# Conditioning products in unsplit fp32, in four 32-column tiles of the array

## The chip, the cores and the metric

The kernel runs on one NeuronCore of a Trainium2 chip. The metric is the device time of one execution in microseconds (us). All inputs and outputs are float32 in the chip's memory.

## What is computed

Two layers of a transformer-like block over 256 context rows and 256 latent rows of width 1024. Each layer runs a gated feed-forward, a mixer and a second feed-forward. All three are modulated and gated by vectors that come from a conditioning product, and this product is what the change is about:

```python
mx = (jax.nn.silu(c) @ w_mod[i] + b_mod[i]).reshape(bsz, N_MOD, d)...   # c: 1 x 1024, w_mod[i]: 1024 x 9216
mc = (jax.nn.silu(c_ctx) @ w_mod[i] + b_mod[i]).reshape(N_MOD, 1, 1, d) # c_ctx: 1024
u  = rmsnorm(h, g_pre) * (1 + scale) + shift                             # rows of mx or mc
y  = (silu(u @ wg) * (u @ wu)) @ wd                                      # wg, wu: 1024 x 2816, wd: 2816 x 1024
h  = h + 0.5 * gate * rmsnorm(y, g_post)
```

There are two conditioning vectors (context and latent), and the weights `w_mod` are 2 x 1024 x 9216 float32 values, 75 MB, of which each is used for two rows only.

## The kernel before

Activations lie with features on the 128 partitions and the 512 rows along the free dimension. Weights come from memory as **panels** of 1024 x 256 values (1 MB, 8 blocks of 128 rows of the inner dimension). A panel is used as two **halves** of 128 columns.

Products are made precise in split form: a value is the sum of a high part in the fast format fp32r and the remainder, also in fp32r. ScalarE copies a half panel to its high part (`weight_hi`, line 85), VectorE subtracts that from the raw panel (`weight_lo`, line 93; GpSimd does it in the mixer), and TensorE multiplies high by high, high by low and low by high (`product_half`, lines 132 to 134), 24 matmuls for a half with 8 blocks.

The conditioning products go the same way, panel by panel, between the halves of the feed-forwards, so that their transfers and splits run beside the weight products. There are 72 panels: 8 in the opening (`opening`), 22 in the up and gate loop of the first feed-forward of layer 0 and 6 in its down products, 22 and 10 in the second feed-forward of layer 0 (for layer 1), and 4 in the down products of the first feed-forward of layer 1. For each half panel:

- SP's queue asks for a panel into the one buffer `raw_mod` (`load_mod`) once both halves of the panel before are split.
- ScalarE makes the high part (`mod_hi`, line 174), once TensorE has finished with the one split buffer `mod_split`; VectorE makes the low part (`mod_lo`, line 180).
- TensorE multiplies (`mod_mm`, line 197): 8 matmuls, one for each block of the inner dimension. The weights are a 128 x 128 slice of `cond`, zero but for four columns: high and low part of the two conditioning vectors. The slice is shifted by four columns for each panel, so that panel n lands on rows 4n to 4n + 3 of the PSUM bank. The moving operand is high and low part of the half panel beside each other, 256 columns.

At the end of a group of panels VectorE adds the sums of high and low parts of the weights into `mod_rows` (`mod_rows_dve`, lines 207 and 209), TensorE turns them with two transposes (`mod_turn_pe`, line 216), and VectorE adds the bias and the two parts of the vectors (`mod_out_dve`, lines 227 and 231).

In the opening there are six stage buffers and the two weight buffers for the eight panels, and four split buffers. TensorE's order there is written out: the first panel, the transposes of x, two panels, then four rounds of column sums of squares and half a panel, parameters, a panel, the norm factors, two panels, the turn. TensorE's warm-up matmuls between stages are at line 415. Two other lines serve the prediction as measures: line 1233 (four products of fp32 operands with 128 x 128 weights for a mean over features, 512 columns in layer 0 and 256 in layer 1) and line 1209 (products in fp32r with 128 x 32 weights), both in the mixer.

## Time and profile before

| what | value |
|---|---|
| median of three runs | 2363.13 us |
| lowest and highest | 2362.87 and 2373.77 us |
| profiled execution, its own time | 2368.33 us |
| profiled execution, span | 2366.6 us |
| mean granted clock of TensorE | 0.964 of full speed |
| TensorE, VectorE, ScalarE, GpSimd busy | 2200.4, 1264.0, 986.5, 230.2 us |
| read from memory | 288.02 MB |

The span is the time from the first to the last instruction of the profiled execution. Busy time is the union of an engine's instructions. A matmul's listed duration includes the time that its results take to leave the array, which the next one overlaps; the time that it holds TensorE is read from one start to the next.

### The profile page before, as it was taken

To read this page: it belongs to the slowest core of one execution; us is meant where nothing else is said; L and a number is where in the kernel's file an instruction comes from. 1 tells how busy PE (TensorE), PEld (TensorE's weight loads), DVE (VectorE), ACT (ScalarE), POOL (GpSimd) and SP (SyncE) were. 2 spreads that over 40 slices of the span, in tenths; PEclk is the share of its full clock that TensorE was granted. 3 is DMA by queue.
4 is the path that set the end of the run, shared out by engine and by line. 5 is a ranking of instruction groups with operands and counts; after the bars stand their busy time and mean duration, and the time that the engine had idled before them with its cause. 6 is when DMAs were issued, how large, how long until landed. Compare 5 with 4: busy or idle time off the path is not lost. (4 is left out here: it accounts for less than half of the span.)

```text
span 2366.6 us, 29334 instructions
## 1 busy us (share of the span) xinstructions
PE 2200.4 (93%) x11949; PEld 1883.8 (80%) x11949; DVE 1264.0 (53%) x1859; ACT 986.5 (42%) x1521; POOL 230.2 (10%) x159
## 2 busy tenths in 40 slices
PE   5999999988988989899999999999998987889998
PEld 5788888876676768688888887888888766778998
DVE  5544444357769743644444445333335578855554
ACT  5444333244465343444443334222324444454443
POOL 0000000033322300100000000000001332300000
PEclk9999999989999989899999998999998999989999
DMA  6445554312242212255554432232422233334553
GB/s 233 146 163 160 161 172 157 98 56 72 91 125 85 76 54 89 89 169 165 165 160 161 159 107 71 89 107 89 157 93 74 72 108 98 108 116 126 187 182 129
DMA packets 282836, 291.09 MB, mean 123 GB/s; under 512 B 8318, under 2 KB 275534, under 8 KB 282702
## 3 DMA queue, kind: packets, MB, share of 16 engines
q1 hardware_dynamic: 281671, 286.95, 37.9%
q10 hardware_dynamic: 1031, 2.28, 0.3%
q8 instruction: 94, 1.54, 0.3%
q14 instruction: 40, 0.33, 0.0%
HBM read 288.02 MB, written 1.18 MB: 122 GB/s over the span
## 5 line engine op out<-in xcount | busy, mean ns | idle before, releaser
L85 ACT ACTIVATE split<-raw 128x1024 fp32r<-128x1024 f32 (+1 forms) x368 | 382.8, 1040 | 929.6 <-PE bank L134 917.4
L93 DVE TENSOR_TENSOR split<-raw,split 128x1024 fp32r<-128x1024 f32 (+1 forms) x304 | 364.2, 1198 | 704.0 <-ACT split L85 703.9
L132 PE MATMUL bank<-uh,split 128*128 128x512 f32 (+1 forms) x1344 | 488.3, 363 | 1.1 <-DVE split L93 1.1
L134 PE MATMUL bank<-uh,split 128*128 128x512 f32 (+1 forms) x1344 | 488.0, 363 | 0.0
L133 PE MATMUL bank<-ul,split 128*128 128x512 f32 (+1 forms) x1344 | 488.0, 363 | 0.0
L134 PEld LDWEIGHTS bank<-uh,split 128*128 128x128 f32 x1344 | 253.7, 189 | 40.1
L132 PEld LDWEIGHTS bank<-uh,split 128*128 128x128 f32 x1344 | 253.8, 189 | 38.2 <-issue 1.5
L133 PEld LDWEIGHTS bank<-ul,split 128*128 128x128 f32 x1344 | 253.8, 189 | 36.8
L132 PE MATMUL bank<-hh,split 128*128 128x256 f32 (+1 forms) x836 | 281.1, 336 | 1.5 <-DVE split L93 1.5
L133 PE MATMUL bank<-hl,split 128*128 128x256 f32 (+1 forms) x836 | 279.5, 334 | 0.0
L134 PE MATMUL bank<-hh,split 128*128 128x256 f32 (+1 forms) x836 | 279.4, 334 | 0.0
L132 PE MATMUL bank<-mix_uh,split 128*128 128x512 f32 (+1 forms) x608 | 233.1, 383 | 26.4 <-POOL split L100 15.9
L134 PE MATMUL bank<-mix_uh,split 128*128 128x512 f32 (+1 forms) x608 | 218.4, 359 | 0.0
L133 PE MATMUL bank<-mix_ul,split 128*128 128x512 f32 (+1 forms) x608 | 218.3, 359 | 0.0
L180 DVE TENSOR_TENSOR mod_split<-raw_mod,mod_split 128x1024 fp32r<-128x1024 f32 x128 | 156.5, 1223 | 63.4 <-ACT mod_split L174 63.3
L197 PEld LDWEIGHTS bank<-mod_split,cond 128*128 128x128 f32 x1152 | 158.4, 194 | 37.8 <-DVE mod_split L180 15.6
L197 PE MATMUL bank<-mod_split,cond 128*128 128x256 f32 x1152 | 164.7, 288 | 24.3 <-DVE mod_split L1965 12.3
L100 POOL TENSOR_TENSOR split<-raw,split 128x1024 fp32r<-128x1024 f32 x64 | 153.9, 2405 | 327.3 <-ACT split L85 327.3
L397 POOL TENSOR_TENSOR res<-res,y 128x256 f32<-128x256 f32 x35 | 26.2, 766 | 1527.8 <-DVE y L382 1527.6
L132 PEld LDWEIGHTS bank<-hh,split 128*128 128x128 f32 x836 | 159.1, 190 | 16.5 <-DVE split L93 1.0
L134 PEld LDWEIGHTS bank<-hh,split 128*128 128x128 f32 x836 | 159.1, 190 | 15.8
L174 ACT ACTIVATE mod_split<-raw_mod 128x1024 fp32r<-128x1024 f32 x128 | 135.1, 1056 | 87.6 <-DMA raw_mod<-in_w_mod 71.8
(231 smaller groups left out, 2969.4 us busy)
## 6 DMA issues: line engine op xcount, KB each, us to landing
raw_mod<-in_w_mod SPq DMA_DIRECT2D x64, 1024.0 KB, 4.8
raw<-in_ffn_w_gate SPq DMA_DIRECT2D x44, 1024.0 KB, 5.2
raw<-in_ffn_w_up SPq DMA_DIRECT2D x44, 1024.0 KB, 5.1
raw<-in_w_in SPq DMA_DIRECT2D x40, 1024.0 KB, 5.1
raw<-in_ffn_w_down SPq DMA_DIRECT2D x32, 1024.0 KB, 5.1
raw<-in_w_out SPq DMA_DIRECT2D x16, 1024.0 KB, 5.0
raw<-in_ffn_w_down SPq DMA_DIRECT2D x16, 768.0 KB, 4.3
decay<-cum_rows SPq DMA_DIRECT2D x48, 256.0 KB, 3.3
```

Of the source, the lines that this page charges most:

```text
L85: ins = K.nc.scalar.activation(K.wh[:, half, 0:kn, :], K.raw[:, slot, 0:kn, half * P:half * P + P], ACT.Copy)
L93: ins = K.nc.vector.tensor_tensor(K.wl[:, half, 0:kn, :], K.raw[:, slot, 0:kn, half * P:half * P + P], r32(K.wh[:, half, 0:kn, :]), ALU.su ...
L100: ins = K.nc.gpsimd.tensor_tensor(K.wl[:, half, 0:kn, :], K.raw[:, slot, 0:kn, half * P:half * P + P], r32(K.wh[:, half, 0:kn, :]), ALU.su ...
L132: K.nc.tensor.matmul(bank[:, 0:tn], K.wh[:, half, k, :], h, start=first and k == 0, stop=False)
L133: K.nc.tensor.matmul(bank[:, 0:tn], K.wh[:, half, k, :], l, start=False, stop=False)
L134: ins = K.nc.tensor.matmul(bank[:, 0:tn], K.wl[:, half, k, :], h, start=False, stop=last and k == kn - 1)
L174: ins = K.nc.scalar.activation(K.mod_split[:, 0], K.raw_mod[:, :, parity * P:parity * P + P], ACT.Copy)
L180: ins = K.nc.vector.tensor_tensor(K.mod_split[:, 1], K.raw_mod[:, :, parity * P:parity * P + P], r32(K.mod_split[:, 0]), ALU.subtract)
L197: ins = K.nc.tensor.matmul(out, cond, split[:, :, k, :], start=h == group_h and k == 0, stop=True, skip_group_check=True)
L397: ins = K.nc.gpsimd.tensor_tensor(K.res[:, j, t0:t0 + CTX], K.res[:, j, t0:t0 + CTX], y[:, j, a:a + CTX], ALU.add)
```

## The change

The conditioning products are no longer split. Their operands are plain fp32, and each of the 8 blocks of the inner dimension goes to one of four column tiles of the array: block k to output rows 32 (k mod 4) to 32 (k mod 4) + 31. The weights are a 128 x 32 slice of `cond`, zero but for the two conditioning vectors; the moving operand is a whole panel, 256 columns. So a panel takes 8 matmuls (in two rounds over the four tiles) instead of 16. A group with more than 16 panels uses both halves of the PSUM bank. The four tiles' partial sums are added in the turn: instead of transposes it multiplies the rows with a 128 x 32 matrix `fold` of four stacked identities. `mod_hi`, `mod_lo`, their buffers and signals go; there are two buffers `raw_mod`, and a panel is asked for when the panel before the last has been multiplied. The opening has eight stage buffers, the panels' order on TensorE is changed a little, and VectorE does the second ahead-of-time weight split after the bias. The rest of the kernel stays.

```diff
@@ -164,71 +164,60 @@
 
 def load_mod(K, sp, w_mod, q, panel):
 
-    sp.wait_ge(K.mod_lo.sem, K.mod_lo.at(2 * panel))
-    sp.dma_start(K.raw_mod[:, :, :], panel_src(w_mod, 0, 8, P * q)).then_inc(K.mod_full.inc(16), 16)
-
-
-def mod_hi(K, act, h, parity, panel):
-    act.wait_ge(K.mod_full.sem, K.mod_full.landed(panel + 1))
-    act.wait_ge(K.mod_mm.sem, K.mod_mm.at(h))
-    ins = K.nc.scalar.activation(K.mod_split[:, 0], K.raw_mod[:, :, parity * P:parity * P + P], ACT.Copy)
-    ins.then_inc(K.mod_hi_done.inc(), 1)
-
-
-def mod_lo(K, dve, h, parity):
-    dve.wait_ge(K.mod_hi_done.sem, K.mod_hi_done.at(h + 1))
-    ins = K.nc.vector.tensor_tensor(K.mod_split[:, 1], K.raw_mod[:, :, parity * P:parity * P + P],
-                                    r32(K.mod_split[:, 0]), ALU.subtract)
-    ins.then_inc(K.mod_lo.inc(), 1)
-
-
-COND_AT = P - 4
-
-
-def mod_mm(K, pe, h, split, group, group_h):
-
-    pe.wait_ge(K.mod_lo.sem, K.mod_lo.at(h + 1))
-    if h == group_h and group:
+    sp.wait_ge(K.mod_mm.sem, K.mod_mm.at(panel - 1))
+    sp.dma_start(K.raw_mod[:, panel % 2], panel_src(w_mod, 0, 8, P * q)).then_inc(K.mod_full[panel % 2].inc(16), 16)
+
+
+COL = 32
+GROUP_ROWS = COL // 2
+
+
+def mod_mm(K, pe, raw, panel, group, first):
+
+
+
+
+
+    if panel == first and group:
         pe.wait_ge(K.mod_row.sem, K.mod_row.at(group))
-    row, parity = 4 * ((h - group_h) // 2), h % 2
+    n = panel - first
+    row, region = 2 * (n % GROUP_ROWS), n // GROUP_ROWS
     for k in range(8):
-        cond = K.cond[:, COND_AT + P * k - row:COND_AT + P * k - row + P]
-        out = K.bank[4][:, parity * 2 * P:(parity + 1) * 2 * P].rearrange("p (w n) -> p w n", w=2)
-        ins = K.nc.tensor.matmul(out, cond, split[:, :, k, :], start=h == group_h and k == 0, stop=True, skip_group_check=True)
+        tile = COL * (k % 4)
+        cond = K.cond[:, COL - 2 + COL * k - row:2 * COL - 2 + COL * k - row]
+        out = K.bank[4][tile:tile + COL, region * 2 * P:(region + 1) * 2 * P]
+        ins = K.nc.tensor.matmul(out, cond, raw[:, k, :], start=n == 0 and k < 4, stop=True, skip_group_check=True)
     ins.then_inc(K.mod_mm.inc(), 1)
 
 
-def mod_rows_dve(K, dve, h, group):
-
-    dve.wait_ge(K.mod_mm.sem, K.mod_mm.at(h + 1))
+def mod_rows_dve(K, dve, panel, panels, group):
+
+    dve.wait_ge(K.mod_mm.sem, K.mod_mm.at(panel + 1))
     dve.wait_ge(K.mod_fold.sem, K.mod_fold.at(group))
-    parts = K.bank[4][:, :].rearrange("p (t w n) -> p w t n", w=2, n=P)
-    rows = K.rows[:, :].rearrange("p (t n) -> p t n", n=P)
-    K.nc.vector.tensor_copy(rows, parts[:, 0]).then_inc(K.mod_row_hi.inc(), 1)
-    dve.wait_ge(K.mod_row_hi.sem, K.mod_row_hi.at(group + 1))
-    K.nc.vector.tensor_tensor(rows, rows, parts[:, 1], ALU.add).then_inc(K.mod_row.inc(), 1)
-
-
-def mod_turn_pe(K, pe, group, bank=7):
+    cols = 2 * P * -(-panels // GROUP_ROWS)
+    K.nc.vector.tensor_copy(K.rows[:, 0:cols], K.bank[4][:, 0:cols]).then_inc(K.mod_row.inc(), 1)
+
+
+def mod_turn_pe(K, pe, panels, group, bank=7):
+
     pe.wait_ge(K.mod_row.sem, K.mod_row.at(group + 1))
-    pe.wait_ge(K.mod_evac.sem, K.mod_evac.at(2 * group))
-    for t in range(2):
-        ins = K.nc.tensor.transpose(K.bank[bank][:, t * P:t * P + P], K.rows[:, t * P:t * P + P], K.ident[:, :])
+    pe.wait_ge(K.mod_evac.sem, K.mod_evac.at(group))
+    for t in range(2 * -(-panels // GROUP_ROWS)):
+        ins = K.nc.tensor.matmul(K.bank[bank][:, t * COL:t * COL + COL], K.rows[:, t * P:t * P + P], K.fold[:, :], start=True, stop=True)
     ins.then_inc(K.mod_fold.inc(), 1)
 
 
 def mod_out_dve(K, dve, layer, q, panels, group, bank=7):
 
     dve.wait_ge(K.mod_fold.sem, K.mod_fold.at(group + 1))
-    turned = K.bank[bank][:, 0:2 * P].rearrange("p (t j i) -> p t j i", t=2, i=4)[:, :, 0:panels, :]
-    out = K.mod[:, layer, q:q + 2 * panels, :].rearrange("p (j t) s -> p t j s", t=2)
-    bias = K.par[:, layer, 0, q:q + 2 * panels].rearrange("p (j t) -> p t j", t=2)
-    for t in range(2):
-        ins = K.nc.vector.tensor_tensor(out[:, t], turned[:, t, :, 0:2], bias[:, t].unsqueeze(2).to_broadcast([P, panels, 2]), ALU.add)
-    ins.then_inc(K.mod_evac.inc(), 1)
-    dve.wait_ge(K.mod_evac.sem, K.mod_evac.at(2 * group + 1))
-    for t in range(2):
-        ins = K.nc.vector.tensor_tensor(out[:, t], out[:, t], turned[:, t, :, 2:4], ALU.add)
+    for region in range(-(-panels // GROUP_ROWS)):
+        n = min(panels - region * GROUP_ROWS, GROUP_ROWS)
+        turned = K.bank[bank][:, region * 2 * COL:(region + 1) * 2 * COL].rearrange("p (t j s) -> p t j s", t=2, s=2)[:, :, 0:n, :]
+        f = q + 2 * region * GROUP_ROWS
+        out = K.mod[:, layer, f:f + 2 * n, :].rearrange("p (j t) s -> p t j s", t=2)
+        bias = K.par[:, layer, 0, f:f + 2 * n].rearrange("p (j t) -> p t j", t=2)
+        for t in range(2):
+            ins = K.nc.vector.tensor_tensor(out[:, t], turned[:, t], bias[:, t].unsqueeze(2).to_broadcast([P, n, 2]), ALU.add)
     ins.then_inc(K.mod_evac.inc(), 1)
 
 
...
@@ -492,12 +481,14 @@
                     for i in range(len(self.streams)):
                         part(half, i, self.halves + n, self.first[p], False)
                 h = self.mod_h + n
-                if n < self.mods:
-                    mod_mm(K, pe, h, K.mod_split, self.mod_group, self.mod_h)
+                if half and n < self.mods:
+                    full = K.mod_full[h // 2 % 2]
+                    pe.wait_ge(full.sem, full.landed(h // 4 + 1))
+                    mod_mm(K, pe, K.raw_mod[:, h // 2 % 2], h // 2, self.mod_group, self.mod_h // 2)
                 if n == 0 and self.mod_group:
-                    mod_turn_pe(K, pe, 0)
+                    mod_turn_pe(K, pe, self.mod_h // 2, 0)
                 if self.mods and n == self.mods + 1:
-                    mod_turn_pe(K, pe, self.mod_group)
+                    mod_turn_pe(K, pe, self.mods // 2, self.mod_group)
                 n += 1
         nth = self.halves + n - 2
         for half in range(2):
...
         for n in range(2 * self.n_panels + 2):
-            p, half, h = n // 2, n % 2, self.mod_h + n
+            p, half = n // 2, n % 2
             if skip <= n < 2 * self.n_panels:
                 weight_hi(K, act, self.panels + p // 2, p % 2, half, self.parts[self.order[p][1]], self.halves + n)
             if n == 2:
                 act.wait_ge(K.pgain_ready.sem, K.pgain_ready.at(1))
-
-            if 1 <= n <= self.mods:
-                mod_hi(K, act, h - 1, 1 - half, (h - 1) // 2)
             if n >= 2 and self.last[p - 1] and self.order[p - 1][0] < 3:
                 j = 2 * self.order[p - 1][0] + half
                 act.wait_ge(K.half_done.sem, K.half_done.at(self.halves + n - 1))
...
         if mods_loop or mods_down:
-            K.raw_mod = mem.enter_context(nc.sbuf_tensor("raw_mod" + tag, [P, 8, 2 * P], F32))
-
-            K.mod_split = mem.enter_context(nc.sbuf_tensor("mod_split" + tag, [P, 2, 8, P], F32R))
-            K.rows = mem.enter_context(nc.sbuf_tensor("mod_rows" + tag, [P, 2 * P], F32))
+            K.raw_mod = mem.enter_context(nc.sbuf_tensor("raw_mod" + tag, [P, 2, 8, 2 * P], F32))
+            K.rows = mem.enter_context(nc.sbuf_tensor("mod_rows" + tag, [P, 4 * P], F32))
         hh = mem.enter_context(nc.sbuf_tensor("hh" + tag, [P, FT, tn], F32R))
         with ExitStack() as under:
             hf = under.enter_context(nc.sbuf_tensor("hf" + tag, [P, FT, tn], F32))
@@ -757,8 +741,10 @@
                     elif not (first and half == 1):
                         product_half(K, pe, K.bank[half], half % 2, 8, lambda k: uh[:, k, :], lambda k: ul[:, k, :], tok,
                                      True, True, 4 * i + half)
-                    if mods_loop:
-                        mod_mm(K, pe, 4 * i + half, K.mod_split, 0, 0)
+                    if mods_loop and half % 2:
+                        panel = 2 * i + half // 2
+                        pe.wait_ge(K.mod_full[panel % 2].sem, K.mod_full[panel % 2].landed(panel // 2 + 1))
+                        mod_mm(K, pe, K.raw_mod[:, panel % 2], panel, 0, 0)
             trip(0, True)
             for i in range(1, pairs):
                 trip(i, False)
...
-            def mod(i, n):
-                if mods_loop:
-                    mod_hi(K, act, 4 * i + n, n % 2, 2 * i + n // 2)
-
             def trip(i, first, last):
                 if not first:
                     weight_hi(K, act, i, 0, 1, 8, 4 * i + 1)
-                mod(i, 0)
...
-        stage = mem.enter_context(nc.sbuf_tensor("stage", [P, 6, 8, 2 * P], F32))
-        split = mem.enter_context(nc.sbuf_tensor("mod_split", [P, 4, 2, 8, P], F32R))
-        K.rows = mem.enter_context(nc.sbuf_tensor("mod_rows", [P, 2 * P], F32))
+        stage = mem.enter_context(nc.sbuf_tensor("stage", [P, 8, 8, 2 * P], F32))
+        K.rows = mem.enter_context(nc.sbuf_tensor("mod_rows", [P, 4 * P], F32))
         block = mem.enter_context(nc.Block(no_gpsimd_drain=True))
         x_tiles = [I["ctx"][0, t * P:(t + 1) * P, :] for t in range(2)] + [I["x"][0, t * P:(t + 1) * P, :] for t in range(2)]
...
             sp.dma_start(cr[8:16, :], I["c"][0].rearrange("(a p) -> a p", p=P)).then_inc(K.cond_in.inc(16), 16)
-            for n in range(2):
-                load_panel(K, sp, n, panel_src(K.w_mod[0], 0, 8, 2 * P * n), 8)
-            for n in range(6):
-                src = panel_src(K.w_mod[0], 0, 8, 2 * P * (n + 2))
+            for n in range(8):
+                src = panel_src(K.w_mod[0], 0, 8, 2 * P * n)
                 sp.dma_start(stage[:, n, :, :], src).then_inc(K.stage_full[n].inc(16), 16)
             for slot, panel in enumerate(following):
-                sp.wait_ge(K.mod_lo.sem, K.mod_lo.at(2 + 2 * slot))
                 load_panel(K, sp, slot, *panel)
 
         @block.gpsimd
...
             line = [[-1, P]]
             select(K.ident[:, :], line, 0, 1, ALU.not_equal, 1.0, n).then_inc(K.const_step.inc(), 1)
+            select(K.fold[:, :], [[-1, COL]], 0, 1, ALU.not_equal, 1.0, n).then_inc(K.fold_step.inc(), 1)
+            for tile in range(1, 4):
+                pool.wait_ge(K.fold_step.sem, K.fold_step.at(tile))
+                nc.gpsimd.affine_select(out=K.fold[:, :], in_=K.fold[:, :], compare_op=ALU.not_equal, fill=1.0, base=-COL * tile,
+                                        pattern=[[-1, COL]], channel_multiplier=1).then_inc(K.fold_step.inc(), 1)
             for d, (step, mult) in enumerate((([[1, P]], -1), (line, 1))):
...
 
             def mods(first, end):
-                for h in range(first, end):
-                    mod_mm(K, pe, h, split[:, h % 4], 0, 0)
-
-            pe.wait_ge(K.const_step.sem, K.const_step.at(9))
+                for panel in range(first, end):
+                    pe.wait_ge(K.stage_full[panel].sem, K.stage_full[panel].landed(1))
+                    mod_mm(K, pe, stage[:, panel], panel, 0, 0)
+
+            pe.wait_ge(K.const_step.sem, K.const_step.at(10))
             pe.wait_ge(K.cond_in.sem, K.cond_in.at(32))
             nc.tensor.transpose(K.bank[0][:, 0:16], cr[:, :], K.ident[0:16, 0:16]).then_inc(K.turn.inc(), 1)
             pe.wait_ge(K.cond_ready.sem, K.cond_ready.at(1))
@@ -1890,18 +1858,17 @@
                 for t in range(TT):
                     ins = nc.tensor.transpose(K.bank[j % 4][:, t * P:t * P + P], xt[:, t, j * P:j * P + P], K.ident[:, :])
                 ins.then_inc(K.turn.inc(), 1)
-            mods(2, 6)
             for i in range(4):
                 pe.wait_ge(K.pair_ready[0].sem, K.pair_ready[0].at(i + 1))
                 sums_pe(K, pe, squares[:, 2 * i, :], FULL, 0, i == 0, i == 3)
-                mods(6 + i, 7 + i)
+                mods(2 + i, 3 + i)
             pe.wait_ge(K.res_ready.sem, K.res_ready.at(4))
             pe.wait_ge(K.res_tail.sem, K.res_tail.at(4))
             params(0)
-            mods(10, 12)
             rstd_pe(K, pe, TOK, 1, 0, CTX)
-            mods(12, 16)
-            mod_turn_pe(K, pe, 0, 3)
+            mods(6, 8)
...
+            act.wait_ge(K.const_step.sem, K.const_step.at(10))
+            cond = K.cond[:, COL - 2:COL - 2 + 8 * COL].rearrange("p (k c) -> p k c", c=COL)[:, :, 0:2]
+            nc.scalar.activation(cond, K.bank[0][:, 0:16].rearrange("p (s k) -> p k s", k=8), ACT.Silu).then_inc(K.cond_ready.inc(), 1)
             for j in range(1, 8, 2):
                 act.wait_ge(K.turn.sem, K.turn.at(2 + j))
                 nc.scalar.activation(K.res[:, j, :], K.bank[j % 4][:, :], ACT.Copy).then_inc(K.res_tail.inc(), 1)
-            mods(2, 6)
             act.wait_ge(K.turn.sem, K.turn.at(9))
             for j in range(8):
                 copied = (K.res_ready, K.res_tail)[j % 2]
                 act.wait_ge(copied.sem, copied.at(j // 2 + 1))
                 ins = nc.scalar.activation(squares[:, j, :], K.res[:, j, :], ACT.Square)
...
             rstd_act(K, act, TOK, 1024, 4, 0)
-            mods(14, 16)
             split_ahead_act(K, act)
 
         @block.vector
         def _(dve):
-            dve.wait_ge(K.turned.sem, K.turned.at(1))
-            cond = K.cond[:, COND_AT:COND_AT + 8 * P].rearrange("p (k c) -> p k c", c=P)
-            ins = nc.vector.tensor_tensor(cond[:, :, 2:4], K.condf[:, :, :], r32(cond[:, :, 0:2]), ALU.subtract)
-            ins.then_inc(K.cond_ready.inc(), 1)
-
-            def mods(first, end):
-                for h in range(first, end):
...
-                    ins = nc.vector.tensor_tensor(split[:, h % 4, 1], raw_mod(h), r32(split[:, h % 4, 0]), ALU.subtract)
-                    ins.then_inc(K.mod_lo.inc(), 1)
-
-            mods(0, 2)
             for j in range(0, 8, 2):
                 dve.wait_ge(K.turn.sem, K.turn.at(2 + j))
                 nc.vector.tensor_copy(K.res[:, j, :], K.bank[j % 4][:, :]).then_inc(K.res_ready.inc(), 1)
-            mods(2, 6)
             for i in range(4):
                 pair_sums_dve(K, dve, squares, FULL, i, 0)
-                mods(6 + i, 7 + i)
-            mods(10, 14)
             rstd_dve(K, dve, TOK, 1, 0)
-            mods(14, 16)
-            mod_rows_dve(K, dve, 15, 0)
-            split_ahead_dve(K, dve)
-            dve.wait_ge(K.turned.sem, K.turned.at(1 + PACKS))
+            mod_rows_dve(K, dve, 7, 8, 0)
+            split_ahead_dve(K, dve, (0,))
+            dve.wait_ge(K.turned.sem, K.turned.at(PACKS))
             mod_out_dve(K, dve, 0, 0, 8, 0, 3)
             pre_gain_dve(K, dve, 0, 0)
+            split_ahead_dve(K, dve, (1,))
     K.end_phase()
 
```

## Rows read from the trace of the kernel before

**Rows 1.** The page: busy us, share of the span, instructions.
```profile
PE 2200.4 (93%) x11949; PEld 1883.8 (80%) x11949; DVE 1264.0 (53%) x1859; ACT 986.5 (42%) x1521; POOL 230.2 (10%) x159
```
**Rows 2.** Window sums: us, engines' busy us, granted clock, DMA share, GB/s; then totals.
```profile
60.00:460.00 400.00, 393.89 (x1969) 332.57 (x1968) 184.95 (x204) 158.91 (x195) 0.00 (x0) 1.00 0.47 153
...
sum 885.00, PE 871.31 PEld 741.04 DVE 399.51 ACT 347.38 POOL 0.00; mean PE 290.44 PEld 247.01 DVE 133.17 ACT 115.79 POOL 0.00
```
**Rows 3.** Timeline, TensorE in the loop: start us, duration us, engine, line, operation.
```profile
201.13 1.11 PE L197 MATMUL bank<-mod_split,cond 128*128 128x256 f32 x8
...
202.07 0.39 PE L132 MATMUL bank<-uh,split 128*128 128x512 f32 x1
...
202.30 0.39 PE L133 MATMUL bank<-ul,split 128*128 128x512 f32 x1
```
**Rows 4.** Waits: who waited for whom, us in total, times, longest.
```profile
PE bank L197 <- DVE mod_split L1965: 12.3, 2, 9.4
PE bank L197 <- DVE mod_split L180: 12.1, 10, 2.5
```
**Rows 5.** The tile raw_mod: duration ns min/median/max, first and last start; landing.
```profile
L174 ACT ACTIVATE mod_split<-raw_mod x128: 1041/1060/1067, 68.1 to 1720.1; 128x1024 fp32r<-128x1024 f32 x128
...
L168 SPq DMA_DIRECT2D raw_mod<-in_w_mod x64: 367/368/582, 55.1 to 1710.4; - x64
...
DMA to landing us min/median/max: 4.7/4.8/8.3
```
**Rows 6.** Timeline, the first two conditioning halves of the first loop.
```profile
71.64 1.23 DVE L93 TENSOR_TENSOR split<-raw,split 128x1024 fp32r<-128x1024 f32 x1 [1.22 <-ACT split L85]
...
73.01 1.11 PE L197 MATMUL bank<-mod_split,cond 128*128 128x256 f32 x8
74.21 1.06 ACT L174 ACTIVATE mod_split<-raw_mod 128x1024 fp32r<-128x1024 f32 x1 [2.61 <-PE bank L197]
...
76.58 1.21 PE L197 MATMUL bank<-mod_split,cond 128*128 128x256 f32 x8 [2.46 <-DVE mod_split L180]
```
**Rows 7.** Line 1233: its durations (ns), and the timeline at its two places.
```profile
L1233 PE MATMUL bank<-yc,ones x16: 377/485/592, 807.9 to 2060.8; 128*128 128x512 f32 x8, 128*128 128x256 f32 x8
...
807.93 3.59 PE L1233 MATMUL bank<-yc,ones 128*128 128x512 f32 x8
...
2059.27 1.89 PE L1233 MATMUL bank<-yc,ones 128*128 128x256 f32 x8
```
**Rows 8.** Timeline where line 1209 begins; PEld is a weight load.
```profile
1861.00 0.39 PE L134 MATMUL bank<-mix_uh,split 128*128 128x512 f32 x1
1861.22 0.39 PE L1209 MATMUL bank<-mix_uh,wdh 128*32 128x512 f32 x1
...
1861.00 0.11 PEld L1209 LDWEIGHTS bank<-mix_uh,wdh 128*32 128x32 f32 x1
```
**Rows 9.** Timeline, a turn between a conditioning half and a weight product.
```profile
356.09 0.38 PE L216 MATMUL bank<-ident,mod_rows 128*128 128x128 f32 x2
356.23 0.48 PE L132 MATMUL bank<-hh,split 128*128 128x512 f32 x1
```
**Rows 10.** Timeline of the opening.
```profile
12.27 2.00 ACT L1920 ACTIVATE mod_split<-raw 128x1024 fp32r<-128x1024 f32 x2 [2.57 <-DMA raw<-in_w_mod]
...
14.73 3.75 PE L197 MATMUL bank<-mod_split,cond 128*128 128x256 f32 x16 [9.36 <-DVE mod_split L1965]
...
18.29 4.85 PE L1891 MATMUL bank<-ident,xt 128*128 128x128 f32 x32
...
27.46 1.14 ACT L1944 ACTIVATE xt<-res 128x512 f32<-128x512 f32 x2
...
31.63 0.95 PE L241 MATMUL bank<-ones,xt 128*128 128x1 f32 x8
...
50.71 0.42 DVE L207 COPY mod_rows<-bank 128x256 f32<-128x256 f32 x1 [3.45 <-PE bank L197]
```
**Rows 11.** Window sums in the opening, columns as in rows 2.
```profile
40.00:55.00 15.00, 8.75 (x58) 8.10 (x56) 8.79 (x15) 7.56 (x9) 0.00 (x0) 0.88 0.00 1
```

More of the change, by code:

```diff
@@ L610, in dve @@
         for n in range(2 * self.n_panels + 2):
-            p, half, h = n // 2, n % 2, self.mod_h + n
+            p, half = n // 2, n % 2
             if skip <= n < 2 * self.n_panels:
@@ L616, in dve @@
                 post_tile_dve(K, dve, (0, self.tok[1]), j + 1, j - 1)
-            if 1 <= n <= self.mods:
-                mod_lo(K, dve, h - 1, 1 - half)
             if n == 0 and self.mod_group:
-                mod_rows_dve(K, dve, self.mod_h - 1, 0)
+                mod_rows_dve(K, dve, self.mod_h // 2 - 1, self.mod_h // 2, 0)
             if n == 1:
@@ L845, in hidden_lo @@
                 ins.then_inc(K.hl_done.inc(), 1)
-            def mod(i, n, first):
-                if mods_loop:
-                    mod_lo(K, dve, 4 * i + n, n % 2)
             def trip(i, first, last):
@@ L853, in trip @@
                     weight_lo(K, dve, 0, 1, 8, 4 * i + 1)
-                mod(i, 0, first)
                 if not first:
@@ L857, in trip @@
                 weight_lo(K, dve, 1, 0, 8, 4 * i + 2)
-                mod(i, 1, first)
                 weight_lo(K, dve, 1, 1, 8, 4 * i + 3)
-                mod(i, 2, first)
                 if not last:
@@ L864, in trip @@
                     weight_lo(K, dve, 0, 0, out.parts[0], 4 * pairs)
-                mod(i, 3, first)
                 product(i, 0)
@@ L1825, in opening @@
         squares = xt[:, :, :].rearrange("p t (h n) -> p (t h) n", n=TOK)
-        def raw_mod(h):
-            panel = K.raw[:, h // 2] if h < 4 else stage[:, h // 2 - 2]
-            return panel[:, :, h % 2 * P:h % 2 * P + P]
         @block.sync
@@ L1913, in params @@
                     ins.then_inc(K.turned.inc(), 1)
-            def mods(first, end):
-                for h in range(first, end):
-                    full = K.raw_full[h // 2] if h < 4 else K.stage_full[h // 2 - 2]
-                    act.wait_ge(full.sem, full.landed(1))
-                    act.wait_ge(K.mod_mm.sem, K.mod_mm.at(h - 3))
-                    ins = nc.scalar.activation(split[:, h % 4, 0], raw_mod(h), ACT.Copy)
-                    ins.then_inc(K.mod_hi_done.inc(), 1)
             for t in range(TT):
@@ L1956, in _ @@
         def _(dve):
-            dve.wait_ge(K.turned.sem, K.turned.at(1))
-            cond = K.cond[:, COND_AT:COND_AT + 8 * P].rearrange("p (k c) -> p k c", c=P)
-            ins = nc.vector.tensor_tensor(cond[:, :, 2:4], K.condf[:, :, :], r32(cond[:, :, 0:2]), ALU.subtract)
-            ins.then_inc(K.cond_ready.inc(), 1)
-            def mods(first, end):
-                for h in range(first, end):
-                    dve.wait_ge(K.mod_hi_done.sem, K.mod_hi_done.at(h + 1))
-                    ins = nc.vector.tensor_tensor(split[:, h % 4, 1], raw_mod(h), r32(split[:, h % 4, 0]), ALU.subtract)
-                    ins.then_inc(K.mod_lo.inc(), 1)
-            mods(0, 2)
             for j in range(0, 8, 2):
@@ L2020, in sp @@
         sp.wait_ge(K.stored.sem, K.stored.at(64))
-FILLER = 64
+FILLER = 142
 def hybrid_block(nc, inputs, out):
@@ L2144, in hybrid_block @@
         K.raw_full = [signal(f"raw_full{n}") for n in range(2)]
-        K.mod_full = signal("mod_full")
-        K.stage_full = [signal(f"stage_full{n}") for n in range(6)]
+        K.mod_full = [signal(f"mod_full{n}") for n in range(2)]
+        K.stage_full = [signal(f"stage_full{n}") for n in range(8)]
         K.bank = [ctx.enter_context(nc.psum_tensor(f"bank{n}", [P, 512], F32)) for n in range(8)]
```

29 lines of the change are left out of this document (9 added, 20 removed).

## Prediction

> **What bounds the kernel now.** The first page gives the shares: TensorE is busy for 93% of the span [rows 1], and no other engine comes near. The window sums over the three stretches with conditioning products (60 to 460, 985 to 1410 and 1680 to 1740 us) then show TensorE busy for 871 of 885 us, at the full granted clock [rows 2]. So there the time is the sum of TensorE's spacings, and work taken off VectorE or ScalarE is worth only the waits that it ends. How long one product holds TensorE is read from starts, since the listed durations (0.39 us) overlap: in the timeline the eight conditioning matmuls of a half panel start at 201.13 and the next weight product at 202.07, 0.94 us later [rows 3]. The list of waits says what the splits cost beyond that: TensorE waited 12.1 us for the conditioning splits in the loops and 12.3 us in the opening [rows 4].
>
> **What is removed.** 128 half panels in the loops (64 DMA issues, two halves each [rows 5]) go, at 0.94 us of TensorE each: 120.3 us, or 1.88 us a panel. The splits on ScalarE (128 in the loops at 1.06 us [rows 5], 16 more in the opening) and the subtractions on VectorE behind them go too. They lie under TensorE's products, except for the 12.1 us [rows 4]. The largest of these waits is 2.5 us: TensorE is done with the first half panel at 73.95, and the second starts at 76.58, behind a split that ScalarE starts at 74.21, because the single split buffer is free only once TensorE has read it [rows 6]. The next product needs a weight split that VectorE started at 71.64 and finished 1.23 us later, so the wait isn't handed on. I take 12.1 us as gained; the bounds are 12.1 and 6, if weight splits were late behind half of them.
>
> **What the new product costs.** An fp32 matmul is not one instruction. The four products of line 1233 over 256 columns stand in the trace as eight, 1.89 us long with 0.38 us for the last alone, so 0.215 us from start to start; those over 512 columns take (3.59 - 0.59)/7 = 0.43 us [rows 7]. So each pass pair costs 0.215 us over 256 columns, one product 0.43 us, and a panel of eight products has sixteen such instructions. The trace of before has no two products in different column tiles, so what they share must be bounded:
> - One after another, nothing shared: 16 x 0.215 = 3.44 us a panel.
> - All four tiles at once: two rounds of 0.43 = 0.86 us.
> - Started in program order: the two instructions of one product use one tile and can't overlap, but the second of tile 0 and the first of tile 1 can. Eight products then take 8 + 1 slots of 0.215 = 1.93 us.
>
> I take the last. For it speaks the streaming rate as well: an ordinary product reads 512 columns from start to start in 0.23 us (202.07 to 202.30 [rows 3]), an fp32 one 256 in 0.215 [rows 7]. Two at once are a rate that the trace shows; four at once would be twice that. The change of width should cost nothing: the narrow products of line 1209 (128 x 32 weights) start 0.22 us after a 128 x 128 one, at 1861.22 after 1861.00, as wide ones do. A narrow weight load takes 0.11 us and lies beneath the matmul [rows 8].
>
> Against the change speaks a rule of the Trainium skill (TensorEngine Tiling (Array Packing), Key Properties): changing the tiling mode drains TensorE. Line 1209 shows no drain, but whether it runs in a column tile the trace doesn't say. By the rule the sum would be the third rival's, 2371 us; going by the row it is 2350.
>
> So the loops change by 64 x (1.93 - 1.88) = +3.2 us, between 64 x (0.86 - 1.88) = -65 and 64 x (3.44 - 1.88) = +100.
>
> **The turn.** Six turns of two transposes (0.14 us, 356.09 to 356.23 [rows 9]) become fp32 products with 32 moving columns: four where a group has 22 panels (twice), two in the other four, each two instructions, 32 in all. The nearest row is eight fp32 instructions of one column in 0.95 us, so at most 0.12 each [rows 10]. 32 x 0.12 - 6 x 0.14 = +3.0 us; its bounds are 0, if the turns fit where weights are awaited anyway, and 3. VectorE's copy and adds get fewer; in the loops they are hidden.
>
> **The opening.** Here TensorE waits for splits, and the memory doesn't bind the end: it moves 1 GB/s after 40 us [rows 11]. Before, the panels' last product ends at 50.7, and VectorE's copy of the rows starts at 50.71 [rows 10]. Rebuilt with my price: the first panel has landed at 12.27, where ScalarE starts on it, and the second, 1 MB like it, comes before TensorE is done with the first. TensorE is slow there (16 conditioning matmuls hold it for 3.56 us, 14.73 to 18.29, nearly twice the loops' price), so I take 3.9 us a panel. The transposes then start at about 20 instead of 18.29, last 4.9 and end at 25. ScalarE squares at once instead of after four splits at 27.46, two squares take 1.14 and an add follows, so the sums start at about 27 instead of 31.63 [rows 10]. Four rounds of sums (0.95 at most) and one panel (1.93) reach 38; parameters and norm factors, two short steps, some 40; two panels 44. That is 6.7 us before 50.7. VectorE's tail loses one pass of 0.42 us over the rows and one pair of small adds, together some 0.7 us. Opening: -7.4 us, estimated. At 0.86 us a panel the same chain ends 15 us earlier; at 3.44 us (and twice that for the first) about 7 us later.
>
> SP's queue gets two panel buffers instead of one and asks for a panel when the one before the last has been multiplied; a transfer lands in 4.8 us (median [rows 5]) and is needed no sooner than a panel later, some 12 us after its issue, so no new wait. The memory is busy for 47% of these stretches [rows 2]. The first two gate and up panels no longer wait for splits, which nobody needed early.
>
> **Sum.** +3.2 - 12.1 + 3.0 - 7.4 = -13.3 us. The profiled execution took 2368.3 us around its span of 2366.6; that is 5.2 us over the median of the runs, 2363.1. I subtract from the median: 2349.8 us. A difference under 0.5% (11.8 us) counts as no change here, so the forecast lies just past that edge.
>
> **Rivals.**
> - *All four tiles at once.* The wait of a product's second instruction doesn't hold up the next tile. -65 - 12.1 + 3.0 - 15 = -89, 2274 us. Against it: twice the streaming rate of any row, and the pairs of instructions [rows 7]. The Trainium skill (TensorE: Matmul & The Clock Gate, Measured speedup vs the span model) has four tiles span one matmul and some 4 ns for each further tile, and so would be this rival.
> - *The change doesn't do what it says: tiles one after another (slower).* TensorE takes up each instruction when the one before has streamed, as everywhere in this trace. +100 - 12.1 + 3.0 + 7 = +98, 2461 us. For it: no row shows an overlap of streams. It decides from the panel's price alone: the gain is gone at 1.93 + 13.3/64 = 2.14 us a panel.
> - *A drain at each change of width.* 0.39 us of a matmul minus the 0.23 us to the next start is 0.16 us of overlap [rows 3, 8]; lost on the way in and out of each panel it is 64 x 0.32 = +21, so 2371 us. Line 1209 speaks against it [rows 8].
> - *The weight loads aren't hidden.* Weights of the next tile are loaded only once the waiting tile has started: 0.11 us on each of eight products [rows 8] would be +56, a quarter of it +14, so 2364 us, up to 2406. For it: loads stand one ahead of the matmuls in these rows, not two.
>
> **Chances.** Pairwise overlap 0.46, its own range 2335 to 2362; four at once 0.19; serial 0.19; drain or unhidden loads 0.16. Faster by over 0.5%: 0.19 and two thirds of 0.46, 0.50. Within 0.5%: the other third and a third of the 0.16, 0.20. Slower: 0.19 and the rest, 0.30. Range: from the four-tile case, 2268, to unhidden loads, 2406; it leaves out the serial case, about 2 in 10.
>
> **What would show it.** The time from the first conditioning matmul of a panel to the next weight product: 1.9 us, against 0.9, 3.4 or 2.3. Inside a panel, starts that come in pairs, 0.215 us apart. TensorE's waits for conditioning splits gone, none for panels in their place. The copy of the rows in the opening at about 44 us. Six turns of 0.4 to 0.8 us. Weight products at 0.23 us as before. The prediction is wrong if the panel's price is elsewhere, or if panels land late.

## The result and the profile after

The changed kernel takes 2306.05 us in the median of 4 runs (2302.89 to 2309.44), the kernel before 2363.49 in as many beside them: ratio 0.9747, interval 0.9717 to 0.9777, 57.4 us less. A second series of the changed kernel gave 2307.19 us, ratio 0.9732 (0.9711 to 0.9754). The profiled execution took 2302.89 us around a span of 2301.2 us. The sign was as forecast, but the forecast, 2349.8 us, was 44 us too high.

The page first, which answers to [rows 1]:
```profile
PE 2149.2 (93%) x11969; PEld 1771.8 (77%) x11969; DVE 1089.0 (47%) x1700; ACT 840.0 (37%) x1376; POOL 229.1 (10%) x164
```
TensorE is as full as before and has 51 busy us less; VectorE and ScalarE lost 175 and 147 us, and neither was or is the bound. The timeline of a panel, which answers to [rows 3]:
```profile
212.00 0.39 PE L132 MATMUL bank<-uh,split 128*128 128x512 f32 x1
212.22 0.39 PE L133 MATMUL bank<-ul,split 128*128 128x512 f32 x1
212.45 0.39 PE L134 MATMUL bank<-uh,split 128*128 128x512 f32 x1
212.77 1.07 PE L189 MATMUL bank<-raw_mod,cond 128*32 128x256 f32 x16
213.77 0.50 PE L132 MATMUL bank<-uh,split 128*128 128x512 f32 x1
214.11 0.40 PE L133 MATMUL bank<-ul,split 128*128 128x512 f32 x1
```
The panel is the 16 instructions that the prediction counted. From the weight product ahead (212.45) to the second one behind it (214.11) 1.66 us pass; two spacings of an ordinary product (212.00 to 212.45) are 0.45, so a panel costs 1.21 us. The prediction read 1.88 us for two halves, from the first conditioning start to the next weight product. Measured edge to edge like the panel, with this line of the kernel before and the 202.30 of [rows 3], a half costs 202.30 - 200.90 - 0.45 = 0.95 us and two cost 1.90:
```profile
200.90 0.39 PE L134 MATMUL bank<-uh,split 128*128 128x512 f32 x1
```
How the 1.21 us are made up stands in the starts of the single instructions of another panel of this trace:

```
start       1st      2nd      3rd      4th
round 1   200.620  200.627  200.633  200.640
round 2   200.860  200.867  200.873  200.880
round 3   201.076  201.082  201.089  201.096
round 4   201.292  201.298  201.305  201.312     next weight product 201.62
```
The rows don't name the tile. But four instructions start within 20 ns, while those of one tile follow each other at 0.215 us (shown below with one tile), so the four are in four tiles. A round follows 0.215 us after the one before (0.24 the first time): each tile has the spacing of [rows 7], and four tiles have it at the same time. Rounds at 0.215 are 0.86 us. The other 0.35 lie at the edges. Into the panel a start is 0.32 us behind the one before, where 0.22 is ordinary (+0.10). The panel lasts 1.00 us to the next weight product (+0.14). The second weight product starts 0.34 behind the first (+0.11).

The window sums of the stages (from one warm-up product of line 415, now 404, to the next): the opening's end, layer 0's two feed-forwards with its mixer between them, then layer 1's first feed-forward, which has the last four panels, and the rest. Columns are as in [rows 2]. Of the kernel before:
```profile
55.13:501.08 445.95, 434.34 (x2236) 370.79 (x2236) 209.68 (x262) 177.15 (x235) 7.52 (x11) 0.98 0.45 145
501.08:972.64 471.56, 423.92 (x2019) 338.80 (x2020) 314.19 (x513) 212.86 (x393) 108.12 (x60) 0.95 0.26 81
972.64:1430.38 457.74, 444.12 (x2297) 380.01 (x2297) 219.04 (x268) 185.03 (x240) 7.47 (x10) 0.98 0.46 150
1430.38:1823.67 393.29, 385.48 (x1846) 323.93 (x1847) 150.63 (x205) 127.97 (x184) 7.76 (x11) 0.98 0.31 99
1823.67:2366.60 542.93, 481.38 (x3347) 440.38 (x3347) 342.29 (x577) 255.75 (x431) 96.64 (x56) 0.95 0.40 125
```
and of the changed kernel:
```profile
48.79:470.82 422.03, 416.00 (x2243) 329.52 (x2244) 141.85 (x201) 120.18 (x179) 7.51 (x11) 0.98 0.46 153
470.82:941.03 470.21, 419.50 (x2020) 335.24 (x2020) 314.51 (x514) 212.62 (x393) 106.93 (x60) 0.95 0.26 81
941.03:1368.05 427.02, 420.15 (x2304) 330.00 (x2305) 141.89 (x199) 119.68 (x176) 7.47 (x10) 0.98 0.48 160
1368.05:1757.99 389.94, 382.68 (x1848) 318.07 (x1849) 140.39 (x194) 119.68 (x176) 7.75 (x11) 0.98 0.31 100
1757.99:2301.20 543.21, 482.63 (x3347) 440.40 (x3347) 341.41 (x577) 255.67 (x431) 96.66 (x56) 0.95 0.39 125
```
The time went where the conditioning is: 6.3 us in the opening, 23.9 and 30.7 in layer 0's feed-forwards (28 and 32 panels), 3.4 with the last four. The stages without a panel moved by -1.4 and +0.3. How far such a stage moves by itself is seen in the second profile of the same kernel, where the mixer's granted clock is 0.93 and not 0.95 and it took 7.6 us more; its window sums:
```profile
471.48:949.30 477.82, 430.17 (x2019) 343.44 (x2020) 313.43 (x513) 213.00 (x393) 107.35 (x60) 0.93 0.26 80
```
Hence prices below are read from starts within a panel, and totals from medians.

The view of the tile raw_mod, which holds the panels of the loops, tells about the waits of [rows 4]; its columns are those of [rows 5]:
```profile
L189 PE MATMUL bank<-raw_mod,cond x1024: 379/379/404, 66.8 to 1659.9; 128*32 128x256 f32 x171
L168 SPq DMA_DIRECT2D raw_mod<-in_w_mod x64: 367/582/1550, 48.8 to 1640.1; - x64
its engine sat idle before it (us, times) until:
  issue: 22.2, 63
...
DMA to landing us min/median/max: 4.9/7.4/11.5
```
No releaser but "issue" is left (63 times 0.35 us on the weight loads, at the edge of a panel): the 12.1 us of [rows 4] are gone, and no wait for a transfer has come in their place, though a panel now lands in 7.4 us and not 4.8 [rows 5]. A turn, which answers to [rows 9]:
```profile
328.48 0.39 PE L134 MATMUL bank<-hh,split 128*128 128x512 f32 x1
328.70 0.97 PE L206 MATMUL bank<-fold,mod_rows 128*128 128x32 f32 x8
329.51 0.48 PE L132 MATMUL bank<-hh,split 128*128 128x512 f32 x1
329.83 0.39 PE L133 MATMUL bank<-hl,split 128*128 128x512 f32 x1
```
Eight instructions take 0.81 us to the next weight product; that is the turn of a group of 22 panels, twice. The opening, which answers to [rows 10]:
```profile
16.75 5.21 PE L1859 MATMUL bank<-ident,xt 128*128 128x128 f32 x32
24.41 1.05 PE L230 MATMUL bank<-ones,xt 128*128 128x1 f32 x8 [2.45 <-DVE xt L239]
25.40 1.07 PE L189 MATMUL bank<-stage,cond 128*32 128x256 f32 x16
...
27.95 1.93 PE L189 MATMUL bank<-stage,cond 128*32 128x256 f32 x16
29.81 1.87 PE L230 MATMUL bank<-ones,xt 128*128 128x1 f32 x8
...
37.13 0.67 PE L1840 MATMUL bank<-ident,pr 120*128 120x120 f32 x2
...
42.54 2.51 PE L189 MATMUL bank<-stage,cond 128*32 128x256 f32 x32
...
45.13 0.43 DVE L198 COPY mod_rows<-bank 128x256 f32<-128x256 f32 x1 [4.64 <-PE bank L189]
```
VectorE's copy of the rows starts at 45.13 where it started at 50.71. But the same panel takes 1.00 us at 25.40 (to the sums at 26.40) and 1.86 at 27.95: the granted clock has gone to its lower level, 1.2 GHz (0.50 of full over 27 to 43 us). Before it fell TensorE had idled 2.45 us and then done one-column sums and a panel in turn. The sums stretch likewise, from 0.99 to 1.80.

### The profile page after: what moved, and what is told of

Its sections match the earlier page's. It is cut to its first block and busy times, and to the rows that moved or that the text cites. A ratio compares the mean times of both kernels' runs of the same rounds, so it can differ in the third digit from the quotient of the medians.

```text
span 2301.2 us, 28935 instructions
## 1 busy us (share of the span) xinstructions
PE 2149.2 (93%) x11969; PEld 1771.8 (77%) x11969; DVE 1089.0 (47%) x1700; ACT 840.0 (37%) x1376; POOL 229.1 (10%) x164
## 5 line engine op out<-in xcount | busy, mean ns | idle before, releaser
L133 PEld LDWEIGHTS bank<-hl,split 128*128 128x128 f32 x836 | 158.7, 190 | 14.8
L132 PEld LDWEIGHTS bank<-mix_uh,split 128*128 128x128 f32 x608 | 118.5, 195 | 50.5 <-issue 19.1
L133 PEld LDWEIGHTS bank<-mix_ul,split 128*128 128x128 f32 x608 | 118.7, 195 | 16.9 <-issue 3.7
L134 PEld LDWEIGHTS bank<-mix_uh,split 128*128 128x128 f32 x608 | 118.2, 194 | 16.1
```

Source lines behind the costliest of these rows:

```text
L132: K.nc.tensor.matmul(bank[:, 0:tn], K.wh[:, half, k, :], h, start=first and k == 0, stop=False)
L133: K.nc.tensor.matmul(bank[:, 0:tn], K.wh[:, half, k, :], l, start=False, stop=False)
L134: ins = K.nc.tensor.matmul(bank[:, 0:tn], K.wl[:, half, k, :], h, start=False, stop=last and k == kn - 1)
```

## The experiments

All kernels compute the whole result. A price of a panel is always taken as above, edge to edge: the start of the second weight product behind the panel, minus the start of the last one ahead, minus two ordinary spacings (0.45).

**Order of the tiles.** If an instruction that waits for its tile holds up all behind it, the four instructions of a tile run one after another and only the borders of tiles overlap: 13 slots of 0.215 us, dearer than the 1.93 of the prediction. If others may pass, the order is nothing.
```
-        tile = COL * (k % 4)
+        tile = COL * (k // 2)
-        ... start=n == 0 and k < 4, stop=True
+        ... start=n == 0 and k % 2 == 0, stop=True
```


> The changed kernel, but neighbouring blocks share a tile: tile k // 2 instead of k mod 4, so TensorE's program has both products of tile 0, then both of tile 1, and so on. Theory A (an instruction that waits for its own tile lets later ones for other tiles go past): the panel still costs four rounds of 0.215 us plus 0.35 for the changes of width, 1.21 us, and the time stays at 2306 us. Theory B (starts come in program order, and the rounds of the changed kernel come from the order alone): the four instructions of a tile run one after another and only the borders overlap, 13 slots of 0.215 = 2.80 us plus 0.35, so 64 x (3.15 - 1.21) = +124 us and some more in the opening, 2430 to 2440 us.

Measured: 2309.22 us (2305.48 to 2313.92), ratio 0.9753 (0.9733 to 0.9773), no different from the changed kernel. The timeline:
```profile
225.97 0.39 PE L134 MATMUL bank<-uh,split 128*128 128x512 f32 x1
226.29 1.09 PE L189 MATMUL bank<-raw_mod,cond 128*32 128x256 f32 x16
227.31 0.50 PE L132 MATMUL bank<-uh,split 128*128 128x512 f32 x1
227.64 0.40 PE L133 MATMUL bank<-ul,split 128*128 128x512 f32 x1
```
The price is 1.67 - 0.45 = 1.22 us, with four starts at 226.287, .300, .313 and .327 (13 ns apart, not 7) and the next four from 226.527. In program order four instructions in a row are for one tile, and still four start together and the price is 1.22, not the 3.15 of strict order: one that waits for its tile lets those for other tiles past.

**Fewer tiles.** All eight blocks in one tile, and in two. Only 32 or 64 rows are then copied and folded.
```
-        tile = COL * (k % 4)
+        tile = COL * (k % 1)        # or k % 2
-        ... start=n == 0 and k < 4, stop=True
+        ... start=n == 0 and k < 1, stop=True        # or k < 2
```


> The changed kernel with all eight products of a panel in one 32-column tile: plain fp32 without the tiling. If the tiles give the gain: sixteen instructions of 0.215 us plus 0.35 for the changes of width, 3.79 us a panel, 64 x (3.79 - 1.21) = +165 us and about +12 in the opening, 2475 to 2490 us, so slower than before by 5%. Rival (the gain is from the splits that are gone, tiles matter little): under 2363 us.

> The changed kernel with the eight products alternating between two tiles. If the price is the longest queue of one tile: eight instructions in a tile, 8 x 0.215 + 0.35 = 2.07 us a panel, 64 x 0.86 = +55 us and +4 in the opening, about 2365 us, the time of the kernel before. If only the first instruction of the next product overlapped (as forecast): 9 slots, 2.29 us, 2380 us.

Measured: one tile 2479.35 us (2477.91 to 2480.79), ratio 1.047 (1.0443 to 1.0498); two tiles 2357.16 us (2352.15 to 2362.73), ratio 0.995 (0.9935 to 0.9966). The timeline with one tile:
```profile
272.99 0.39 PE L134 MATMUL bank<-uh,split 128*128 128x512 f32 x1
273.31 3.64 PE L189 MATMUL bank<-raw_mod,cond 128*32 128x256 f32 x16
...
277.22 0.40 PE L133 MATMUL bank<-ul,split 128*128 128x512 f32 x1
```
and two:
```profile
240.13 0.39 PE L134 MATMUL bank<-uh,split 128*128 128x512 f32 x1
240.44 1.92 PE L189 MATMUL bank<-raw_mod,cond 128*32 128x256 f32 x16
...
242.63 0.40 PE L133 MATMUL bank<-ul,split 128*128 128x512 f32 x1
```
The prices are 4.23 - 0.45 = 3.78 and 2.50 - 0.45 = 2.05 us. With 1.21 for four tiles they lie on one line: 0.215 us for each instruction of the fullest tile (16, 8, 4: 3.44, 1.72, 0.86) and 0.33 to 0.35 whatever the number of tiles. That second term is not a cost of an instruction, of a tile or of a weight load in a tile.

**Half the changes of width.** Panels two at a time, after every fourth half panel of weights.
```
-                if half and n < self.mods:
+                if n % 4 == 3 and n < self.mods:
+                    for panel in (h // 2 - 1, h // 2):
...                     (wait for the panel, mod_mm as before)
```


> The changed kernel with the panels multiplied two at a time, after every fourth half in the loops: the same 64 panels, but 32 changes of width there and back instead of 64. Theory A (0.35 us of a panel's 1.21 is the change between 128- and 32-column weights, each way): 32 x 0.35 = 11 us less, 2295 us. Theory B (the 0.35 us belongs to each panel, its first weight load and last result): no change, 2306 us. Theory C (both buffers are now free at the same time, so panels land late and TensorE waits): slower than 2306 us, with waits for raw_mod in the list.

Measured: 2290.16 us (2286.66 to 2295.26), ratio 0.9673 (0.9653 to 0.9694), against 0.9747 and 0.9732 of the changed kernel. Its timeline:
```profile
125.45 0.39 PE L134 MATMUL bank<-uh,split 128*128 128x512 f32 x1
125.77 1.93 PE L189 MATMUL bank<-raw_mod,cond 128*32 128x256 f32 x32
127.63 0.50 PE L132 MATMUL bank<-uh,split 128*128 128x512 f32 x1
127.97 0.40 PE L133 MATMUL bank<-ul,split 128*128 128x512 f32 x1
```
Two panels cost 2.52 - 0.45 = 2.07 us, which is 1.72 and one 0.35: the 0.35 is paid by the change from full-width to 32-column products and back, once for however many products there are between. 32 fewer are 32 x 0.35 = 11 us; the ratios say 14 to 17, but each carries some 5 us of uncertainty, which 11 fits.

Is it the width, or only the change from fp32r to unsplit fp32, which comes with it in every one of these kernels? The turn tells. It is unsplit fp32 too, but its weights have all 128 columns. Its eight instructions cost 329.83 - 328.48 - 0.45 = 0.90 us, and a turn with four costs 403.20 - 402.30 - 0.45 = 0.45:
```profile
402.30 0.39 PE L134 MATMUL bank<-hh,split 128*128 128x512 f32 x1
...
403.20 0.39 PE L133 MATMUL bank<-hl,split 128*128 128x512 f32 x1
```
Half the instructions at half the price leave nothing for the edges, so the change of type alone costs nothing here, and the 0.35 us go with the width. The Trainium skill (TensorEngine Tiling (Array Packing), Key Properties) says that a change of the tiling mode drains TensorE; these rows fit that, and give the price of it here.

**The splits' load put back.** Was the gain in the loops also the idle time of ScalarE and VectorE? The changed kernel got two copies on ScalarE and two subtractions on VectorE, each on [128, 512], behind every weight split of the gate and up loops, on tiles that nothing else needs there.
```
+            def filler_hi():
+                if mods_loop:
+                    for part in range(2):
+                        act.wait_ge(K.act_step.sem, K.act_step.own())
+                        nc.scalar.activation(K.sq[:, 0, :], K.res[:, part, :], ACT.Copy).then_inc(K.act_step.inc(), 1)
...                     (filler_lo on VectorE likewise, with a subtraction)
```


> The changed kernel with work put back at the places of the conditioning splits in the two up and gate loops: per half two copies of 512 columns on ScalarE (some 1.1 us) and two subtractions on VectorE (some 1.4 us) on data that nobody waits for, 88 halves. Theory A (the splits lay under TensorE's products and only their waits cost): within 3 us of the changed kernel. Theory B (load on these engines or their memory ports slows TensorE's weight products, or delays the weight splits): 88 x 0.1 to 0.3 us, 9 to 26 us more.

Measured: 2301.72 us (2300.31 to 2305.94), ratio 0.9715 (0.9697 to 0.9733), beside 0.9732 for the unchanged copy. In the window sums:
```profile
50.42:472.45 422.03, 414.86 (x2243) 328.27 (x2244) 197.97 (x290) 170.99 (x267) 7.51 (x11) 0.98 0.46 153
```
VectorE and ScalarE have 56 and 51 busy us more than the 141.85 and 120.18 of the changed kernel, where the change had taken 68 and 57 off, and the stage takes the same 422.03 us. Load of about this size on the two engines costs TensorE nothing here, so the splits had cost only what TensorE waited for them.

**The opening.** Two panels are multiplied while the squares are awaited (2.45 us idle ahead of the sums), and none is left behind the norm factors.
```
+            mods(2, 4)
             for i in range(4):
...
-                mods(2 + i, 3 + i)
+                mods(4 + i, 5 + i)
...
             rstd_pe(K, pe, TOK, 1, 0, CTX)
-            mods(6, 8)
```


> The changed kernel with another order of TensorE in the opening: two panels straight after the transposes, then each round of sums with one panel, and no panel left after the norm factors. In the trace of the changed kernel TensorE idles 2.4 us after the transposes, the granted clock is at half from 27 to 44 us, panels there take 1.86 us instead of 1.00, and the last two panels and the turn come after the norm factors. Theory A (the order costs the idle stretch and with it the clock): the next stage starts at 40 to 43 us instead of 48.8, so 6 to 9 us less. Theory B (the clock stays low whatever fills the stretch): only the two late panels are saved, 2 to 3 us less. Theory C (something else ends the opening, the weight split on ScalarE and VectorE or the parameters): under 1 us.

Measured: 2298.00 us (2296.60 to 2305.01), ratio 0.9702 (0.9682 to 0.9723). The next stage starts at 45.61 us, not 48.79: 3.2 us. The ratios make it 7 us (0.9702 beside 0.9732), with intervals that overlap. The clock was at its lower level from 27.6 us, as before, though TensorE idled only 0.59 us ahead of the sums, so the gain is of the order alone, and the idle stretch isn't what takes the clock down.

**Both.** The edits of the last and of the paired panels in one kernel.

> Both edits together: panels two at a time in the loops, and the opening's order. If they add: 16 us from the pairs (measured on another chip against the kernel before) and what the opening alone gives, 2282 to 2290 us.

Measured: 2286.09 us (2284.67 to 2290.22), ratio 0.9649 (0.9631 to 0.9667); and in a second series, as

> Pairs and the opening's order, once more as the base of the next: 2286 us, between 2281 and 2291.

2283.64 us (2281.08 to 2284.85), ratio 0.9646 (0.9626 to 0.9665). The changed kernel was run again under its own expectation in between:

> The changed kernel itself, on the same chip as the three below, as their base: 2306 us, between 2302 and 2310.

Measured: 2307.19 us (2302.75 to 2312.37).

**The clock of the opening.** To the last kernel full-width warm-up products were added: one between each round's sums and its panel, and four behind the parameters, where TensorE waits for the norm factors.
```
                 sums_pe(K, pe, squares[:, 2 * i, :], FULL, 0, i == 0, i == 3)
+                warm_pe(K, 1, 6)
                 mods(4 + i, 5 + i)
...
             params(0)
+            warm_pe(K, 4, 6)
```


> The same with full-width fp32 matmuls on constants, which nobody reads, in the opening: one in each round of sums, four while TensorE waits for the norm factors. In the trace of the one above the clock falls to half at 29 us, while TensorE does narrow panels and one-column sums, and panels take 1.86 instead of 1.00 us, sums 1.80 instead of 0.98. Theory A (the wide work holds the clock): three panels and rounds at full clock, 4 to 5 us less, less four times 0.43 us of added work, so the next stage starts 2 to 4 us earlier. Theory B (the clock falls all the same): the added work takes 4 x 0.43 to 4 x 0.86 us, the next stage starts 2 to 3 us later.

Measured: 2282.10 us (2279.78 to 2285.37), ratio 0.9644 (0.9623 to 0.9664). Without them, in the second series above, the window sums:
```profile
20.00:43.00 23.00, 20.12 (x161) 13.86 (x159) 6.35 (x10) 10.12 (x18) 0.00 (x0) 0.66 0.73 259
```
and the timeline:
```profile
28.12 1.93 PE L189 MATMUL bank<-stage,cond 128*32 128x256 f32 x16
...
45.78 0.76 PE L404 MATMUL bank<-tri,ident 128*128 128x256 f32 x1 [2.30 <-PEq L1785]
```
With them, the window sums:
```profile
20.00:43.00 23.00, 19.25 (x181) 13.38 (x179) 9.18 (x19) 10.46 (x19) 0.00 (x0) 0.94 0.74 260
```
and the timeline:
```profile
28.48 1.07 PE L189 MATMUL bank<-stage,cond 128*32 128x256 f32 x16
...
41.70 0.77 PE L404 MATMUL bank<-tri,ident 128*128 128x256 f32 x1 [2.52 <-PEq L1785]
```
The granted clock over 20 to 43 us is 0.94 and not 0.66, the panels keep their 1.00 us, and the next stage starts 4.1 us earlier, though TensorE has 16 instructions more to do. In the medians it is 1.5 us, with intervals that overlap: the opening's gain is shown, the whole kernel's is not.

## Why the prediction was right in sign and wrong in size

The forecast sign came true, but not by the way that the prediction preferred: by its price the loops would have become 3 us slower, and the gain lay in waits and in the opening. Measured, most of the gain is in the price of a panel, by the mechanism of a rival that had a chance of 0.19. That the value lies inside the range says little, since the range runs from 2268 to 2406 us. (Its lower end is called the four-tile case, which by the prediction's own sum is 2274.)

- **The price of a panel** is the step that failed, in the part "What the new product costs": "Started in program order". It was 1.93 us; measured is 1.21. The second instruction of a product does wait for its tile, but the next tile's do not wait behind it: 0.86 us for the instructions, the rival of all four tiles at once. The prediction took two at once because no row had a higher rate. But nothing in the trace bounded the rate; it was only the highest one seen. In the sum this is 64 x (0.86 - 1.93) = -68 us.
- **"The change of width should cost nothing"** failed as well, the other way: 0.35 us a panel, 64 x 0.35 = +22 us; the third rival, which put 0.32 on it, had the size. Line 1209 [rows 8] was the wrong witness. Its operands are in fp32r. That such products run in no column tile would fit it. The Trainium skill (PSUM — Partial Sum Buffer, The four PSUM rules) notes that float32r matmuls force the mask of all column groups. No run here shows it: fp32r in column tiles wasn't tried. So in the terms of the prediction the loops change by 64 x (1.21 - 1.88) = -42.9 us, not +3.2; with both prices taken edge to edge, by 64 x (1.21 - 1.90) = -44.2. Two rivals held at once, which none of the cases did.
- **What is removed**: the two halves were costed from starts, and the splits at nothing but their waits. Both held, with small errors of size. 1.88 should have been 1.90, as above. And the list of waits counts idle time alone: in [rows 6] the second half starts at 76.58 where 73.95 was due, 2.63 us lost and not 2.46. Read so from the starts, the ten waits cost 13.5 us and not 12.1. The waits for splits in the loops are gone and none came; with the splits' load put back the stage takes as long.
- **The turn**: predicted +3.0 us. Measured 0.81 us twice, and 0.36 for the four instructions of a shorter turn, of which there are three in the loops, less 5 x 0.14: +2.0.
- **The opening**: predicted -7.4, measured -6.3 (48.79 for 55.13), with the copy of the rows at 45.13 where "about 44" stood. That is luck, since the steps are off both ways. The first two panels cost 1.86 us each where 3.9 was taken, so the transposes start at 16.75, not 20, though TensorE waited 1.02 us for the second panel, which the prediction had landing in time. The sums start at 24.41, not 27. One panel then costs 1.00 us and not 1.93; from about 27 us on the granted clock is 1.2 GHz, panels cost 1.86 and the sums 1.80 where 0.95 was taken, and the rounds end at 37.13, not 38. Parameters and norm factors, put at 2 us, take 5.4 (to 42.54). The prediction had no step for the clock, and with it the four-tile price gave little of the rival's 15 us.
- **No new wait for panels**: right for the loops, in spite of the longer landing.
- **The sum** with what was measured: -44.2 - 13.5 + 2.0 = -55.7 us for the loops, where the three stages with panels lost 23.9 + 30.7 + 3.4 = 58.0. With the opening it is -62.0, against -65.4 between the two spans and -57.4 in the medians. The 2.3 us that the stages lost beyond their terms are not assigned; single executions differ by more in a stage that nothing touched (7.6 us in the mixer).
- **The rivals.** Tiles one after another is what one tile does (3.78 us, 2479 us in all, 2461 forecast); four tiles don't. Unhidden weight loads of narrow tiles: the two terms above leave nothing for them.

## What to carry to other kernels

fp32 products with few stationary columns are cheap in four column tiles: count the instructions of the fullest tile, 0.215 us each over 256 columns, in either of the two orders tried. Add 0.35 us for each excursion from full-width products into tiles and back, and therefore gather such products: with panels in pairs and the opening reordered this kernel came to 2286 and 2284 us in two series, some 20 us below the change itself. Take a row as witness for a cost only if it has the same type and shape. And where the highest rate in the rows is only what happened to be issued, don't take it for a limit: give the case beyond it its full chance.

## What the runs showed of the hardware that was not expected

- TensorE starts instructions for free column tiles past one that waits for its tile: with k // 2 as the tile, the four first starts are 13 ns apart. Since instructions of one tile follow at 0.215 us, these must be the first, fifth, ninth and thirteenth of the panel in the program. In the changed kernel they are 7 ns apart. The Trainium skill (TensorE: Matmul & The Clock Gate, The mechanism) has matmuls start strictly in program order, some 4 ns apart; for these fp32 pairs the rows show otherwise, and the measurement decides.
- Over 20 to 43 us TensorE was busy for 20.12 of 23 us, mostly with one-column sums and 32-column panels in turn, and yet the granted clock was 0.66 of full over that stretch; warm-up products over the full width between them, 0.61 us in each round, held it at 0.94 with 19.25 us busy.
